# Differential attention maps in two products instead of three; queries and keys moved by transfers that GpSimd issues

## The reference

```
sc = einsum("bqhcd,bkhcd->bchqk", q, k) * (64 ** -0.5)   # c = 2 maps, each of depth 64
p = softmax(sc, axis=-1)
a = p[:, 0] - lam * p[:, 1]                              # differential attention
o = einsum("bhqk,bkhd->bqhd", a, v)
```

## Time and profile before

| | us |
|---|---|
| median of 3 runs | 1184.05 (1182.55 to 1184.13) |
| the profiled execution | 1184.92 |
| its span, first to last instruction | 1183.1 |
| PE busy | 1170.2 (99%) |
| DVE busy | 727.9 (62%) |
| ACT busy | 580.9 (49%) |
| POOL busy | 95.3 (8%) |

### The profile page before, as it was taken

One profiled execution on the slowest core, in us unless ns is written; L12 is line 12 of the kernel. 1 busy time (PEld: TensorE's weight loads), 2 busy tenths in 40 slices (PEclk: granted clock), 3 DMA queues, 4 the chain that ended last, 5 costly groups with the idle time before them and its releaser, 6 DMA issues.

```text
span 1183.1 us, 14666 instructions
## 1 busy us (share of the span) xinstructions
PE 1170.2 (99%) x5524; PEld 978.2 (83%) x5524; DVE 727.9 (62%) x839; ACT 580.9 (49%) x754; POOL 95.3 (8%) x129
## 2 busy tenths in 40 slices
PE   8999999999999999999999999999999999999997
PEld 6888888888888888888888888888888888888886
DVE  5675556656764955764656555565746567658554
ACT  6554445454555644574545454444444444445442
POOL 2400002000000000011100101102011002000000
PEclk8999999999999999999999999999999999999999
DMA  9977676644646555455767666666766666454541
GB/s 357 242 224 247 204 242 214 231 160 161 243 150 247 178 191 201 147 210 173 246 212 227 219 202 227 207 219 203 244 200 186 231 204 214 144 202 151 199 154 72
DMA packets 77224, 242.08 MB, mean 205 GB/s; under 512 B 26048, under 2 KB 43072, under 8 KB 51696
## 3 DMA queue, kind: packets, MB, share of 16 engines
q1 hardware_dynamic: 75024, 233.87, 58.4%
q0 software_dynamic: 1856, 7.38, 2.3%
q10 hardware_dynamic: 288, 0.08, 0.0%
HBM read 221.37 MB, written 8.39 MB: 194 GB/s over the span
## 4 chain that ended last, share of the span: by engine, by line
PE 97%; DVE 1%; DMA 1%; ACT 0%; SPq 0%; issue 0%; DVEq 0%; ACTq 0%
PE acc L460 90%; PE bank_x L624 2%; PE bank_y L577 1%; DMA raw<-weights 1%; PE bank_x L620 1%; PE bank_y L566 1%; PE bank_x L608 1%; PE bank_y L593 0%; PE bank_x L593 0%; PE bank_y L573 0%; PE bank_x L521 0%; PE bank_y L521 0%; DVE w_lo L1008 0%; ACT w_hi L726 0%; DVE resid L1297 0%; SPq L305 0%
## 5 line engine op out<-in xcount | busy, mean ns | idle before, releaser
L460 PE MATMUL acc<-w_hi,act_hi 128*128 128x512 f32 x1560 | 617.1, 396 | 3.9 <-DVE w_lo L1008 3.9
L460 PE MATMUL acc<-w_lo,act_hi 128*128 128x512 f32 x1560 | 609.2, 390 | 0.0
L1008 DVE TENSOR_TENSOR w_lo<-raw,w_hi 128x2048 fp32r<-128x2048 f32 x195 | 449.4, 2307 | 187.7 <-ACT w_hi L726 187.5
L726 ACT ACTIVATE w_hi<-raw 128x2048 fp32r<-128x2048 f32 x195 | 373.7, 1917 | 296.6 <-PE acc L460 288.6
L460 PE MATMUL acc<-w_hi,act_lo 128*128 128x512 f32 x1560 | 418.4, 390 | 0.0
L460 PEld LDWEIGHTS acc<-w_hi,act_hi 128*128 128x128 f32 x1560 | 294.0, 188 | 61.7 <-issue 4.3
L460 PEld LDWEIGHTS acc<-w_hi,act_lo 128*128 128x128 f32 x1560 | 293.3, 188 | 62.2 <-DVE act_lo L1026 0.4
L460 PEld LDWEIGHTS acc<-w_lo,act_hi 128*128 128x128 f32 x1560 | 293.9, 188 | 57.3
L733 ACT ACTIVATE unit<-acc,pre_r 128x512 f32<-128x512 f32 x78 | 49.4, 685 | 125.5 <-PE acc L460 122.2
L405 POOL TENSOR_TENSOR rope_c<-unit,cst 128x256 f32<-128x256 f32 (+1 forms) x19 | 14.1, 740 | 789.5 <-ACT unit L733 656.5
L748 ACT ACTIVATE probs<-scores,negm 128x256 f32<-128x256 f32 (+1 forms) x80 | 36.4, 458 | 29.3 <-DVE negm L1096 25.3
(11 more groups left out here) (173 smaller groups left out, 617.3 us busy)
## 6 DMA issues: line engine op xcount, KB each, us to landing
raw<-weights SPq DMA_DIRECT2D x195, 1024.0 KB, 5.0
qk_raw<-postg SPq DMA_DIRECT2D x176, 64.0 KB, 2.3
p_moved<-p_blocks SPq DMA_DIRECT2D x16, 256.0 KB, 5.5
probs<-p_moved SPq DMA_DIRECT2D x64, 64.0 KB, 2.0
mix<-rpb POOLq DMA_DIRECT2D x32, 64.0 KB, 17.9
postg<-post_g POOLq DMA_DIRECT2D x2, 1024.0 KB, 8.7
resid<-x_perm POOLq DMA_DIRECT2D x2, 1024.0 KB, 8.8
p_moved<-p_blocks SPq DMA_DIRECT2D x16, 128.0 KB, 5.0
```

What stands on the lines that cost most here:

```text
L460: m = nc.tensor.matmul(tiles[t][:, :], a[:, kt, t * P:(t + 1) * P], w[:, buf, kk * NB:(kk + 1) * NB], start=(kt == 0 and a is act_hi and w ...
L726: nc.scalar.activation(w_hi[:, at % SPLIT, :], raw[:, at % RAW, :], ACT.Copy).then_inc(S["hi_ready"], 1)
L1008: nc.vector.tensor_tensor(w_lo[:, at % SPLIT, :], raw[:, at % RAW, :], w_hi[:, at % SPLIT, :].bitcast(F32), ALU.subtract).then_inc(S["lo_r ...
```

## The change

- `gather` moves from SP's program to POOL's and takes one part (0 queries, 1 keys) instead of both: 16 transfers of 32 KB for each part, 32 for a unit. Ahead of each sixteen, POOL waits for the part's own semaphore and runs one `tensor_tensor` of one column (`tick`).
- DVE transposes queries at slot 6 and keys at slot 10 (`TURNS`; 8 and 10 in a layer's first body). The semaphores are split in two (`q_turned`, `k_turned`, `q_in`, `k_in`).
- In POOL's program the order is now rotate queries, gather queries, rotate keys, gather keys, and for D rotate the shared keys after that.
- B units: `split_q` and its clearing go. The 64 rows of a map's high query part stand in `q_hi`, and the low query part stands in the other 64 rows, which were zero. `both_k` holds the high keys of a map in both halves of the partitions, and the low keys in both halves. A map is two products in place of three, at each of two row tiles.
- ACT's high parts for B are six instructions instead of three, all after a wait for both parts; DVE's low parts are six instead of three, map 0 at half 2 and map 1 at half 3. PE waits for each map's parts by themselves.
- D: the shared keys are transposed, and split, at half 3 instead of half 4; low query parts are made at half 2.

```diff
-TURN = 10
+TURNS = (6, 10)
+FIRST_TURNS = (8, 10)
...
+            def gather(index, blk):          # in POOL's program
+                pool.wait_ge(S[("q", "k")[blk] + "_turned"], index + 1)
+                pool.wait_ge(S["ticked"], CREDIT + 2 * index + blk)
+                pool.tensor_tensor(tick[:, :], cst[:, 0:1], cst[:, 1:2], ALU.add).then_inc(S["ticked"], 1)
+                for a in range(QUADS):
+                    for j in range(QUADS):
+                        pool.dma_start(qk_raw[j * QUAD:(j + 1) * QUAD, a, blk, :], blocks[blk][a * QUAD:(a + 1) * QUAD, j, :]).then_inc(
+                            S[("q", "k")[blk] + "_in"], 16)
...
             def score_map(u, j, c):
+                pe.wait_ge(S["qk_ready"], 2 * split_units(u) + c + 1)
...
-                    for n, (a, b) in enumerate(PARTS):
+                    for part in range(2):
                         m = nc.tensor.matmul((Y, X)[c][:, t * SEQ:(t + 1) * SEQ].rearrange("p (t a c) -> p t a c", t=NT, a=QUADS),
-                                             split_q[:, c, a, t * UH + j, :],
-                                             keys_of((k_hi[:, :, :], k_lo)[b], j), start=(n == 0), stop=(n == len(PARTS) - 1))
+                                             q_hi[:, c, t * UH + j, :], keys_of(both_k[:, c, part, :, :], j),
+                                             start=(part == 0), stop=(part == 1))
...
             def split_qk_hi(u):
+                act.wait_ge(S["q_in"], PART_DMAS * u.index + PART_DMAS)
+                if u.kind != "A" and u.kind != "W":
+                    act.wait_ge(S["k_in"], PART_DMAS * u.index + PART_DMAS)
                 if u.kind == "B":
                     for c in range(2):
+                        mine, other = (slice(64 * r, 64 * r + 64) for r in (c, 1 - c))
+                        nc.scalar.activation(by_quads(q_hi[mine, c, :, :]), raw_quads(0, mine), ACT.Copy).then_inc(S["qk_hi"], 1)
+                        nc.scalar.activation(both_k[other, c, 0, :, :], qk_raw[mine, :, 1, :], ACT.Copy)
+                        nc.scalar.activation(both_k[mine, c, 0, :, :], qk_raw[mine, :, 1, :], ACT.Copy).then_inc(S["qk_hi"], 1)
...
+            def split_both_lo(u, c):          # DVE, half 2 for map 0, half 3 for map 1
+                mine, other = (slice(64 * r, 64 * r + 64) for r in (c, 1 - c))
+                dve.wait_ge(S["qk_hi"], hi_count(u) + 2 * c + 1)
+                nc.vector.tensor_tensor(by_quads(q_hi[other, c, :, :]), raw_quads(0, mine),
+                                        by_quads(q_hi[mine, c, :, :].bitcast(F32)), ALU.subtract)
+                dve.wait_ge(S["qk_hi"], hi_count(u) + 2 * c + 2)
+                for rows in (other, mine):
+                    m = nc.vector.tensor_tensor(both_k[rows, c, 1, :, :], qk_raw[mine, :, 1, :],
+                                                both_k[mine, c, 0, :, :].bitcast(F32), ALU.subtract)
+                m.then_inc(S["qk_ready"], 1)
...
-                        if s == TURN and turned_next(layer, u) is not None:
-                            turn_qk(layer, turned_next(layer, u))
+                        at = FIRST_TURNS if u is None else TURNS
+                        if s in at and turned_next(layer, u) is not None:
+                            turn_part(layer, turned_next(layer, u), at.index(s))
```

More of the change, by code:

```diff
@@ L152, in build @@
         mix = sb("mix", [P, NT, D_MODEL])
-        with nc.sbuf_tensor("split_q", [P, 2, 2, NT * UH, P], F32R) as split_q:
+        with nc.sbuf_tensor("both_k", [P, 2, 2, QUADS, NT * UH * QUAD], F32R) as both_k:
             pass
@@ L196, in build @@
         warm = sb("warm", [P, 1])
+        tick = sb("tick", [P, 1])
         std = sb("std", [P, NT])
@@ L244, in build @@
                  "y_sq y_scaled y_sum y_var y_std y_rdy "
[L245 removed]
+                 "rs_v rs_s rs_rdy tanh_done gate_u gate_done").split()
         S = {n: sem(n) for n in names}
@@ L288, in turns, with hi_count @@
             return f - 1
+        def hi_count(u):
+            return 2 * split_units(u) + (0 if u.kind == "A" else 2 * (u.index - 2) if u.kind == "B" else 4)
         def split_units(u):
@@ L416, in _ @@
                 for u, _, _ in loops(pool, layer):
-                    if u is None or u.kind == "A":
+                    if u is None:
                         continue
-                    turns = ((0, NB), (1, NB), (2, 2 * HEAD)) if u.kind == "D" else ((0, NB), (1, NB))
-                    for k, (blk, cols) in enumerate(turns):
+                    turned = ((0, NB), (1, NB), (2, 2 * HEAD)) if u.kind == "D" else ((0, NB), (1, NB))
+                    for k, (blk, cols) in enumerate(turned):
+                        if u.kind == "A":
+                            gather(u.index, blk)
+                            continue
                         pool.wait_ge(S["proj_ready"], PROJ0[layer] + 3 * u.body - 2 + k)
@@ L425, in _ @@
                         rotate(u, k, blk, cols, HEAD // 2 if layer == 0 else HEAD)
[L426 to L430, removed]
+                        if blk < 2:
+                            gather(u.index, blk)
                 if layer == 0:
-                    pool.wait_ge(S["qk_in"], QK_DMAS * UNITS[0])
+                    pool.wait_ge(S["q_in"], PART_DMAS * UNITS[0])
+                    pool.wait_ge(S["k_in"], PART_DMAS * UNITS[0])
                     pool.dma_start(postg[:, :], post_g[0].partition_broadcast(P)).then_inc(S["postg_in"], 16)
@@ L630, in attention @@
                     return
-                if u.kind == "D" and h == 4:
+                if u.kind == "D" and h == 3:
                     turn_shared_k(u)
@@ L802, in attention @@
                         order_pT(u, j)
-                if h == 2:
+                if h == (1 if u.kind in ("B", "D") else 2):
                     split_qk_hi(u)
-                if h == 4 and u.kind == "D":
+                if h == 3 and u.kind == "D":
                     act.wait_ge(S["k_full"], 1)
@@ L1054, in split_qk_lo @@
-            def split_qk_lo(u):
-                for blk in range(2):
-                    dve.wait_ge(S["qk_hi"], 2 * split_units(u) + blk + 1)
-                    if u.kind == "B" and blk == 0:
-                        for c in range(2):
-                            rows = slice(64 * c, 64 * c + 64)
-                            m = nc.vector.tensor_tensor(by_quads(split_q[rows, c, 1, :, :]), raw_quads(0, rows),
-                                                        by_quads(split_q[rows, c, 0, :, :].bitcast(F32)), ALU.subtract)
-                    elif blk == 0 or u.kind == "D":
+                    dve.wait_ge(S["roped"], CREDIT + 2 * (index - 2) + 1 + blk)
@@ L1065, in split_qk_lo @@
+            def split_qk_lo(u):
+                dve.wait_ge(S["k_in"], PART_DMAS * u.index + PART_DMAS)
+                for blk in range(2):
+                    dve.wait_ge(S["qk_hi"], hi_count(u) + blk + 1)
+                    if blk == 0 or u.kind == "D":
                         m = nc.vector.tensor_tensor(by_quads(q_lo[:, blk, :, :]), raw_quads(blk),
@@ L1217, in attention @@
                     return
-                if h == 3 and u.kind != "G":
+                if u.kind == "B" and h in (2, 3):
+                    split_both_lo(u, h - 2)
+                if h == (2 if u.kind == "D" else 3) and u.kind not in ("B", "G"):
                     split_qk_lo(u)
-                if h == 4 and u.kind == "D":
+                if h == 3 and u.kind == "D":
                     dve.wait_ge(S["k_split"], 1)
```

39 lines of the change are left out of this document (13 added, 26 removed).

## The result

The changed kernel takes 1193.12 us (median of 6 runs, 1188.32 to 1193.59) against 1183.02 for the kernel before on the same chip: a ratio of 1.0076, 95% interval [1.0066, 1.0086]. It is slower by 10.1 us by the medians and 9.0 by the ratio, where +0.7 was forecast and 1189.5 was the end of the range. The profiled execution took 1193.57 us, its span is 1191.8.

A forecast was written before the change was run, and what follows sets the result against it. PE, busy almost throughout, was taken as the bound. Products -3.84, index 3's wait +4.3 and index 2's third head +0.25 summed to +0.7 us, a median going from 1184.05 to 1184.8, range 1180.4 to 1189.5.

The forecast's parts named there:

- part 4: Units other than index 3: no waits, A and W some 4 us to spare; only index 2's third head costs 0.25 us.
- part 3: Index 3's keys: transposition, tick, sixteen issues and landing put them at 310.6, so PE waits 4.3 us once.
- one for one: PE's stream: each instruction removed is time saved and each wait added is time lost, in equal amount.
- index 2's third head: Queries turned at slot 6 make the combination end at 275.8 where PE wants it at 275.55: 0.25 us lost.
- Part 1: PE's maps: one product of 0.12 us fewer in each of 32 cases, 3.84 us saved.
- Part 2: Index 3's first map: with doubled splitting PE waits if keys land after 306.3; at their old time, 2.5 us lost.
- Chunk 3: DVE's subtraction at index 3: binds only for keys beyond 307.8 and by less than the combination, adding nothing.
- Landing: Index 3's keys: a small POOL transfer lands 4.5 us after issue, bounds 2.3 and 6.0.
- index 2 no wait: Index 2: keys land at 228.9 and may come as late as 229.1, so no wait, 0.2 us to spare.
- D no wait: Unit D: key transfers end at 981.1, before the first rotation is due at 982.44; forecast cost 0.
- Rival B: POOL's sixteen issues bound: index 3 waits 6.8, index 2 and D 2.2 each, 1191.7 us; three slower rivals together 0.27.
- C: Rival: POOL cannot write descriptors while DVE subtracts; keys up to 4.6 us later, 1189.4 us; three slower rivals together 0.27.

The follow-up runs named there:

- e7: The changed kernel with 16 of the 32 bias transfers (heads 4 to 7) left out: 1183.4 us, ratio 1.0005 to the kernel before.
- e13: The kernel of e7 once more, for a profile at the full clock: 1183.43 us in its single run.
- e10: The whole changed kernel, with the bias transfers of heads 4 to 7 issued behind index 0's keys: 1184.08 us, ratio 1.0009 to before.
- e1: The changed kernel, with index 0's 32 transfers issued by SP instead of POOL: 1185.04 us, ratio 1.0018 to the kernel before.
- e4: The change's movement (POOL issues, queries at slot 6) with before's splitting and three products a map: 1192.01 us, ratio 1.0075 to before.
- e9: e3, and for index 3 alone SP moves queries at slot 6, keys at slot 10, queries split first: 1179.62 us, ratio 0.9973 to before.
- e12: The kernel of e9 once more, beside other kernels on one chip: 1179.83 us, ratio 0.9966 to the kernel before.
- e3: The change's two products and splitting, with before's movement (SP, both parts at slot 10, 64 KB transfers): 1182.19 us, ratio 0.9995 to before.

## Why the prediction was wrong

The sum was missed by 8.3 us, 1193.12 against 1184.8 (9.4 by the change from before, 10.1 against 0.7), and one step of it is the cause: **part 4, "A and W units take the keys after the queries ... and their x falls some 4 us into it: some 4 us to spare ... Cost nothing"**. PE wanted index 0's score at 88.92 + 1.07 = 89.99 and needs 2.42 us behind the keys, so they could land at 87.6. With the 4.5 us that part 3 gave to a landing, they would have been there at 77.4 + 4.5 = 81.9, and the slack was even more than stated. They needed 18.7. The landing was priced as in an idle queue for every unit, and the prediction said so itself ("No small transfer of POOL's in an idle queue is in this trace"), without asking what stands in that queue when index 0 comes. The trace of before had the answer: the last bias transfer is issued at 43.6, and their landing, which the prediction left out, was up to 29.3 us there:

```profile
DMA to landing us min/median/max: 9.3/17.9/29.3
```

That is a queue busy until about 72.9, when index 0's queries have been issued and its keys begin. Before, nobody used it then, and SP's own transfers for index 0 began at 73.1, just behind it. e7, e13 and e10 show that the bias rows are the cause: 16 transfers out of the way, or later, give 9.0 to 9.7 us back. That they act through POOL's queue alone is not shown: in e1 SP's transfers, outside that queue, were slow at index 0 as well (9.0 us).

The second thing the prediction had at nothing is what follows a long wait: it took a wait as time lost "one for one", and the slow clock behind this one cost 1.7 us more (2.7 in e4). With both, the sum closes: -3.84 + 10.2 at index 0 + 3.6 at index 3 + 0.2 at index 2's third head = +10.2, against 10.1 measured by the medians and 9.0 by the ratio.

Point by point:
- Part 1, the products: right. A map is four products in place of six, and where index 3 does not wait (e9 and e12) the kernel is 3.3 and 3.6 us below before by the medians: about the 3.84, less what the early queries cost at index 2.
- Part 2, the deadline of index 3: right to 0.2 us (table). Chunk 3 was to bind beyond 307.8 by less than the combination and to add nothing: it made PE wait first (1.58), and 1.18 were left for the combination, so the 4 us that were to show before the transposition stood in two places. The end of the chain is the same.
- Part 3: the key transposition 1.15 earlier, right. `tick` held behind DVE's subtraction, right: it ended 304.93 - 302.76 = 2.2 after the transposition, forecast 2.4, and a memset in its place took 0.10. The Trainium skill ("SBUF — State Buffer", who interferes with whom) states that a DVE instruction with two SBUF inputs contends with a GpSimd instruction that reads SBUF and not with one that only writes it; both rows agree. Issues 0.49 us each, forecast 0.50. Landing 4.0 from the last issue, forecast 4.5. The keys came 7.8 us into the unit instead of 8.6, and the wait was 3.6 instead of 4.3. The price from the Trainium skill's "DMA: Bandwidth & Descriptors" (an estimate of 2.1 us for 32 KB on the gpsimd path) is met by none of the medians: 4.3 us over 320 transfers, with weights moving all the time; the minimum, 1.7, is near it.
- Part 4, index 2 no wait: right (ACT starts at 236.34 without one), in part by luck: only 0.2 us was to spare with a tick of 2.4, and the tick there took 0.19. D no wait: right; its tick took 0.19 us and its keys' issues ended 3.6 us ahead of the first rotation. Index 2's third head: its distance is 282.78 - 273.26 = 9.52, and 9.32 in e3, which moves no queries there (271.62 - 262.30): 0.2 us where 0.25 was forecast. Index 0: wrong.
- Rival B named the slow queue, but gave it to weight traffic and to the issue rate, at index 2, 3 and D; its 1191.7 came near for a reason that did not occur. C did not occur: issues stayed at 496 to 525 ns at index 3 beside DVE's subtraction, and at 561 at most over all 352.

Without index 0 the forecast stands within its range. That e10 is 0.7 us above before, the sum's own figure, is in part luck: its wait at index 3 was 3.35 and not 4.3, so by its own waits it should be 0.3 below, and its interval reaches from 0 to +2.1. A result above the range had about 0.1 of the chances.

## What to carry to other kernels

When transfers are moved to another queue, list everything that this queue already holds, by its issues and by its landings, at each moment when the new ones arrive, the first unit above all; a queue that the kernel used only at the start is not idle when its last issue is done. Then ask of every unit when its data are wanted, and use one measured distance (here first map to transposition) to check the slack in each variant. And a gain on the bound engine is paid back where the work that feeds it gets longer or comes later: of 3.84 us of products index 3 took 2.8 back with the keys at their old time (e3) and 3.6 with the change's. Long waits are to be priced with the slow clock behind them.

## What the runs showed of the hardware

- Small-row transfers of POOL's drained slowly while weights came in: 32 bias transfers of 64 KB in rows of 256 bytes were issued in 19.6 us, the first landed at 34.9 and the last at 77.9, 1.4 us each (1.7 in e13; e10's late sixteen 1.5). Index 0's 32 KB transfers issued behind them took 15.6 and 12.7 us in the median instead of 4.3; SP's, in a queue of their own, 9.0 instead of 2.5.
- After PE's 8.5 us without work the granted clock was at its lower level (1.2 GHz), and stayed there for some 3.5 us after PE had resumed, a loss of 1.7 us. After 5.9 us (e4) it stayed there for some 5.7 us, a loss of 2.7: the shorter wait had the larger price. The waits of 1 to 2 us at index 3 had none (1.00 from 326 to 338).
- SP's issues cost by the transfer, not by its bytes: sixteen took 10.01 us at 32 KB and at 64 KB. POOL's sixteen of 32 rows took 7.86, 0.49 us each, and its 32 bias transfers of 256 rows 19.62, 0.61 each; those at index 3 stayed at 496 to 525 ns beside DVE's subtraction.
- A POOL instruction of one column is held by DVE's subtraction only if it reads: 2.15 us as a `tensor_tensor`, 0.10 as a memset. (The two differ in their operation too; no run has the same one without its reads.) For the keys of index 0, index 2 and D, where DVE had a pause of 0.4, 1.0 and 0.9 us behind the transposition, the reading one took 0.19.
